# Three fp32 transformer blocks on one core: a second layer begun per channel tile, a convolution slab moved to the matmul engine, and the first network one tile later

## The reference

```python
def first_block(x, ...):
    for i in range(2):                        # layer 0: Hyena, layer 1: RWKV7
        h = _rmsnorm(x, norm_mix_g[i])
        if i % 2 == 0: y = _hyena_mixer(h, ...)
        else:          y, v_first = _rwkv7_mixer(h, v_first, ...)
        x = x + y
        h = _rmsnorm(x, norm_ffn_g[i])
        x = x + _conv_ffn(h, ff_w_up[i], ff_conv_w[i], ff_conv_b[i], ff_w_down[i])
    return _rmsnorm(x, final_norm_g)

def _hyena_filter(...):                       # three layers of 64 channels, then taps for 2 x 1024 channels
    hdn = sin(fq * (z @ w1 + b1)); hdn = sin(fq * (hdn @ w2 + b2)); hdn = sin(fq * (hdn @ w3 + b3))
    k = hdn @ w4; k = k * exp(-t * deltas)

def _rwkv7_mixer(h, ...):
    xx = 0.5 * (h[t - 1] + h[t + 1]) - h      # token difference
    xr, xw, xk, xv, xa, xg = [h + xx * mu[j] for j in range(6)]      # six mixtures
    r = xr @ w_r; k = xk @ w_k; v = xv @ w_v; a = sigmoid(a0 + (xa @ a1) @ a2); ...

def third_block(x, c, ...):
    mod = silu(c) @ w_ada + b_ada             # 6 x 1024 scales and shifts, depends on c alone
    q, k, v, iq, ik, iw, ca, cg = split(h @ w_in)
    attn = dsa_sparse_attention(...)          # 8 heads, 4 blocks of 128 queries, up to 512 keys, top 128 kept
    y = depthwise causal convolution, 31 taps, 512 channels, of ca * sigmoid(cg)
    conv = silu(layer_norm(y))
    x = x + gt1 * (concat[rms_norm(attn), rms_norm(conv)] @ w_out)
    x = x + gt2 * (relu(h2 @ w_ff1) ** 2 @ w_ff2)
```

## Times and profile before

| | us |
|---|---|
| three runs | 3405.93, 3418.65, 3418.45 (median 3418.45) |
| the profiled execution | 3414.19 |
| its span (first to last instruction) | 3412.4 |
| outside the span | 1.8 |
| mean granted clock of PE | 0.956 of full |
| PE busy | 3210.9 (94%) |
| POOL, ACT, DVE busy | 1240.9, 1140.2, 1582.5 |

### The profile page before, as it was taken

How to read it: one execution, slowest core, us unless ns; L and a number is a source line. 1 busy time by engine, 2 the same in 40 slices (tenths; PEclk the granted TensorE clock), 3 DMA queues, 4 the chain that set the end, 5 groups by cost and what they waited for, 6 DMA issues and landing times.

```text
span 3412.4 us, 62787 instructions
## 1 busy us (share of the span) xinstructions
PE 3210.9 (94%) x25578; PEld 2444.1 (72%) x25578; DVE 1582.5 (46%) x2350; ACT 1140.2 (33%) x1619; POOL 1240.9 (36%) x641
## 2 busy tenths in 40 slices
PE   8999999879899999999998999989997998989999
PEld 5757888748688887877766765458885774548887
DVE  6755553284355545777031412353243577436060
ACT  5414433212433333443233223132223235632221
POOL 3323444324034413444433321024442266604443
PEclk9999999989899999999998999999998797699999
DMA  3213333313000002555322321123332120013333
GB/s 134 81 37 93 93 97 102 96 56 99 1 3 3 3 27 73 186 184 184 105 96 74 93 70 54 52 66 95 97 99 68 56 69 31 1 56 99 93 98 99
DMA packets 73073, 266.36 MB, mean 78 GB/s; under 512 B 8207, under 2 KB 8218, under 8 KB 72704
## 3 DMA queue, kind: packets, MB, share of 16 engines
q1 hardware_dynamic: 72000, 260.32, 24.0%
q0 software_dynamic: 896, 3.52, 0.3%
HBM read 261.71 MB, written 2.10 MB: 77 GB/s over the span
## 4 chain that ended last, share of the span: by engine, by line
PE 75%; issue 10%; DVE 7%; POOL 4%; ACT 3%; DMA 0%; SPq 0%; POOLq 0%; DVEq 0%; ACTq 0%
PE gp L388 53%; PE gp L1226 4%; POOL w_low L357 4%; PE gp L314 2%; PE gp L2156 2%; PE gp L2648 2%; PE aux L1343 1%; PE gp L1971 1%; PE aux L1980 1%; PE aux L1226 1%; PE gp L2616 1%; PE aux L565 1%; DVE aux L2812 1%; PE aux L1221 1%; PE aux L2564 1%
## 5 line engine op out<-in xcount | busy, mean ns | idle before, releaser
L357 POOL TENSOR_TENSOR w_low<-ring,w_high 128x1024 fp32r<-128x1024 f32 x397 | 955.2, 2407 | 1774.8 <-ACT w_high L326 1774.8
L326 ACT ACTIVATE w_high<-ring 128x1024 fp32r<-128x1024 f32 x397 | 420.2, 1060 | 1342.5 <-PE gp L388 1291.1
L388 PE MATMUL gp<-ffn_h,w_high 128*128 128x512 f32 x2432 | 757.1, 393 | 12.3 <-DVE ffn_h L418 5.1
L388 PEld LDWEIGHTS gp<-ffn_h,w_high 128*128 128x128 f32 x2432 | 454.7, 188 | 123.3 <-POOL w_low L357 12.0
L388 PE MATMUL gp<-ffn_h,w_low 128*128 128x512 f32 x1216 | 474.7, 390 | 0.0
L388 PE MATMUL gp<-ffn_high,w_high 128*128 128x512 f32 x928 | 362.7, 391 | 9.8 <-POOL w_low L357 9.8
L388 PE MATMUL gp<-ffn_low,w_high 128*128 128x512 f32 x864 | 337.6, 391 | 0.0
L388 PE MATMUL gp<-ffn_high,w_low 128*128 128x512 f32 x864 | 337.2, 390 | 0.0
L388 PEld LDWEIGHTS gp<-ffn_h,w_low 128*128 128x128 f32 x1216 | 229.1, 188 | 48.1
L2084 DVE TENSOR_TENSOR arena<-arena 128x512 f32<-128x512 f32 x64 | 152.6, 2384 | 200.6 <-ACTq L163 200.6
L388 PE MATMUL gp<-in_h,w_high 128*128 128x512 f32 x768 | 239.0, 393 | 4.5 <-DVE in_h L416 4.5
(11 more groups left out here) (466 smaller groups left out, 5144.2 us busy)
## 6 DMA issues: line engine op xcount, KB each, us to landing
ring<-in_weights SPq DMA_DIRECT2D x437, 512.0 KB, 3.6
H<-in_ada SPq DMA_DIRECT2D x48, 512.0 KB, 4.2
X<-in_x SPq DMA_DIRECT2D x4, 512.0 KB, 7.5
out_x<-X SPq DMA_DIRECT2D x8, 256.0 KB, 4.6
arena<-in_sm POOLq DMA_DIRECT2D x1, 1024.0 KB, 5.0
cst<-in_cst SPq DMA_DIRECT2D x1, 756.0 KB, 9.8
arena<-in_hy_f_w POOLq DMA_DIRECT2D x1, 512.0 KB, 5.5
arena<-in_hy_delta POOLq DMA_DIRECT2D x1, 512.0 KB, 6.1
```

What stands on the lines that cost most here:

```text
L326: nc.scalar.activation(w_high[:, slab % PARTS, :], ring[:, slab % RING, :], ACT.Copy).then_inc(high_ready, 1)
L357: nc.gpsimd.tensor_tensor(w_low[:, slab % PARTS, :], ring[:, slab % RING, :], w_high[:, slab % PARTS, :], ALU.subtract).then_inc(low_ready, 1)
L388: last = nc.tensor.matmul(gp[:, t.bank, :], wt[:, slab % PARTS, w], x(k), start=(k == 0 and q == 0), stop=(k == sum(kt) - 1 and q == 2))
```

## The change

Four edits, in four places:

- **A, start.** The sum of squares is read ahead of tile 2 rather than tile 1, the filter network stands ahead of tiles 3, 4, 5 rather than 2, 3, 4. ACT splits two slabs ahead of the root rather than one.
- **B, `down1`.** The squares go to free tiles of `arena` (48 and on) rather than to `H`, and the last four products of `w_ada` stand behind the first four residual additions, one each.
- **C, RWKV7 start.** DVE does for each channel tile its norm, its difference (one copy of two columns rather than two) and its part of mixture 0; PE waits for each tile apart.
- **D, block 3.** The convolution's slab 2 goes to PE: 31 products 128x512 with a diagonal matrix each, which ACT makes from the identity (8 at a time), summed in PSUM bank 2 of `gp`. Four stand ahead of unit 0, two behind each of units 0 to 7, one behind each of units 8 to 18. ACT moves the sum out at unit 20. The list of taps of ACT and POOL is shorter (52 entries rather than 83, POOL's additions 51 rather than 81), one behind each unit, and the scores have two banks rather than three.

```diff
...
             def beside(j):
-                if j == 1:
+                if j == 2:
                     pe.wait_ge(cst_in, 16)
                     folded_norm_pe(pe, arena_tiles(hX1), False)
-                if 2 <= j <= 4:
-                    i = j - 2
+                if 3 <= j <= 5:
+                    i = j - 3
                     if i:
                         pe.wait_ge(f_sin, i)
...
             for t in loop_tiles(act, STAGE["hy_in"], a, body=24):
                 nxt = t.j + 1
-                split_ahead_act(act, t)
+                if t.j != 1:
+                    split_ahead_act(act, t)
                 if t.j == 0:
+                    split_ahead_act(act, Tile(t.st, 1, None, t.body))
                     act.wait_ge(cst_in, 16)
                     root_act(act, a)
...
-                if 2 <= nxt <= 4:
-                    act.wait_ge(f_arg, nxt - 1)
-                    nc.scalar.activation(f_h[nxt - 2], f_t[0], ACT.Sin).then_inc(f_sin, 1)
+                if 3 <= nxt <= 5:
+                    act.wait_ge(f_arg, nxt - 2)
+                    nc.scalar.activation(f_h[nxt - 3], f_t[0], ACT.Sin).then_inc(f_sin, 1)
...
-                if 2 <= t.j + 1 <= 4:
-                    filter_layer(t.j - 1)
+                if 3 <= t.j + 1 <= 5:
+                    filter_layer(t.j - 2)
...
-            squares_beside_act(act, a, f"down{layer}", Xk, Hk, x_wait(act, n_act))
+            squares_beside_act(act, a, f"down{layer}", Xk, arena_tiles(ffX2), x_wait(act, n_act))
...
-            if layer:
-                for j in range(2 * F1T, MODS):
-                    ada_dve(dve, v, j)
-            residual_dve(dve, v, f"down{layer}", sq=Hk)
+            residual_dve(dve, v, f"down{layer}", sq=arena_tiles(ffX2), beside=(lambda j: ada_dve(dve, v, 2 * F1T + j) if j < MODS - 2 * F1T else None) if layer else None)
...
+            for t in loop_tiles(pe, st):
+                bank_wait(pe, t)
+                slab_wait(pe, st.slab0 + t.j)
+                for k in range(DT):
+                    pe.wait_ge(rw_xx, t.j * DT + k + 1)
+                    last = nc.tensor.matmul(gp[:, t.bank, :], ring[:, (st.slab0 + t.j) % RING, k * P:(k + 1) * P],
+                                            arena[:, buf(t.j) + k, :], start=(k == 0), stop=(k == DT - 1))
+                last.then_inc(slab_done, 1)
...
-            pre_norm_dve(dve, v, "norm_mix", DT)
-            v.settle()
-            dve.wait_ge(h_ready, n_dve.h)
+            root_dve(dve, v)
             for i in range(DT):
                 xx, h = arena[:, wXX + i, :], H[:, i, :]
+                nc.vector.scalar_tensor_tensor(out=h, in0=X[:, i, :], scalar=pcol("norm_mix", DT + i), in1=root[:],
+                                               op0=ALU.mult, op1=ALU.mult).then_inc(h_ready, 1)
+                dve.wait_ge(h_ready, n_dve.h + i + 1)
                 v.go(nc.vector.tensor_tensor(xx[:, 1:S - 1], h[:, 0:S - 2], h[:, 2:S], ALU.add))
-                v.go(nc.vector.tensor_copy(xx[:, 0:1], h[:, 1:2]))
-                v(nc.vector.tensor_copy(xx[:, S - 1:S], h[:, S - 2:S - 1]))
+                v(nc.vector.tensor_copy(xx[:, 0:S:S - 1], h[:, 1:S - 1:S - 3]))
                 v(nc.vector.scalar_tensor_tensor(out=xx, in0=xx, scalar=0.5, in1=h, op0=ALU.mult, op1=ALU.subtract))
+                mixed_into(0, i).then_inc(rw_xx, 1)
...
             def score(i):
                 u, n = A.units[i], A.u0 + i
-                if n >= 3:
-                    pe.wait_ge(at_exp, n - 2)
+                if n >= A.banks:
+                    pe.wait_ge(at_exp, n - A.banks + 1)
...
+        DIAGS = 8
+        DIAG_UNIT = lambda u: min(4 + 2 * (u + 1), 20) if u < 8 else min(20 + u - 7, CONVK)
...
+            def tap_products(lo, hi):
+                for k in range(lo, hi):
+                    if k == 0:
+                        pe.wait_ge(cv_pad, 3)
+                    pe.wait_ge(cv_diag, k + 1)
+                    nc.tensor.matmul(gp[:, 2, :], DIAG(k), PE_PAD[:, k:k + S], start=(k == 0), stop=(k == CONVK - 1),
+                                     skip_group_check=True).then_inc(cv_prod, 1)
+            attention_pe(pe, DSA, lambda u: tap_products(0 if u < 0 else DIAG_UNIT(u - 1), DIAG_UNIT(u)))
...
-            attention_act(act, DSA, lambda i: taps(20 + 2 * i, 22 + 2 * i))
-            taps(20 + 2 * len(dsa_units), len(TAPS))
+            def diagonals(lo, hi):
+                for k in range(lo, hi):
+                    if k >= DIAGS:
+                        act.wait_ge(cv_prod, k - DIAGS + 1)
+                    nc.scalar.activation(DIAG(k), ident, ACT.Copy, scale=tap(2, k)).then_inc(cv_diag, 1)
+            def beside(u):
+                taps(20 + u, 21 + u)
+                diagonals(DIAG_UNIT(u) + 2, DIAG_UNIT(u + 1) + 2 if DIAG_UNIT(u + 1) < CONVK else CONVK)
+                if DIAG_UNIT(u - 2) == CONVK > DIAG_UNIT(u - 3):
+                    act.wait_ge(cv_prod, CONVK)
+                    a.go(nc.scalar.activation(arena[:, dCV + 2, :], gp[:, 2, :], ACT.Identity, bias=pcol("b_dw3", 2)))
+                    a.tell(cv_ready)
+            diagonals(0, DIAG_UNIT(0) + 2)
+            attention_act(act, DSA, beside)
+            taps(20 + len(dsa_units), len(TAPS))
...
```

More of the change, by code:

```diff
@@ L638, in h_before, with residual_dve @@
             return before
-        def residual_dve(dve, v, name, bias=None, body=8, sq=None):
+        def residual_dve(dve, v, name, bias=None, body=8, sq=None, beside=None):
             st = STAGE[name]
@@ L652, in residual_dve @@
                 v.tell(drained[t.bank], x_ready)
+                if beside:
+                    beside(t.j)
                 if sq and t.j == DT - 2:
@@ L1958, in build, with __init__, attention_pe @@
         class Attention:
[L1961 removed]
+            def __init__(self, units, p, pt, scale, u0, eye, banks=3):
+                self.banks = banks
                 self.units, self.p, self.pt, self.scale, self.u0, self.eye = units, p, pt, scale, u0, eye
[L1964 removed]
+        def attention_pe(pe, A, beside=None):
             def score(i):
                 u, n = A.units[i], A.u0 + i
[L1967 to L1968 removed]
+                if n >= A.banks:
+                    pe.wait_ge(at_exp, n - A.banks + 1)
                 if u.chosen:
                     pe.wait_ge(sel_ready, u.chosen)
[L1971 removed]
+                nc.tensor.matmul(gp[:, n % A.banks, 0:u.nk], u.q, u.k, start=True, stop=False, skip_group_check=True)
                 lo, m = u.mask
[L1973 removed]
+                nc.tensor.matmul(gp[:, n % A.banks, lo:u.nk], A.eye, m, start=False, stop=True,
                                  skip_group_check=True).then_inc(at_score, 1)
@@ L1985, in attention_pe @@
             score(1)
+            if beside:
+                beside(-1)
             for i, u in enumerate(A.units):
@@ L1997, in attention_pe @@
                     values(i - 1)
+                if beside:
+                    beside(i)
             values(len(A.units) - 1)
@@ L2015, in exp @@
                     act.wait_ge(at_tr, n - 1)
-                nc.scalar.activation(A.p(n)[:, 0:u.nk], gp[:, n % 3, 0:u.nk], ACT.Exp, bias=stat(n, 1),
+                nc.scalar.activation(A.p(n)[:, 0:u.nk], gp[:, n % A.banks, 0:u.nk], ACT.Exp, bias=stat(n, 1),
                                      scale=A.scale if u.root is None else u.root,
@@ L2476, in build @@
         TAPS = [("tap", 0, k, POOL_PAD) for k in range(OWN_TAPS, CONVK - 1)]
-        for _i, _pad in ((3, PAD), (2, POOL_PAD)):
-            TAPS += [("first", _i, CONVK - 1, _pad)] + [("tap", _i, k, _pad) for k in range(CONVK - 1)]
+        TAPS += [("first", 3, CONVK - 1, PAD)] + [("tap", 3, k, PAD) for k in range(CONVK - 1)]
+        cv_diag, cv_prod = f_comb, hy_ready
         def three_pool(pool, g):
@@ L2510, in three_pool @@
                 y = arena[:, dCV + i, :]
-                if (kind, i) == ("first", 3):
-                    pool.wait_ge(cv_used, m)
-                    g.tell(cv_ready)
-                    product(2, POOL_PAD)
-                    g.tell(cv_pad)
-                if (kind, i) == ("first", 2):
+                if m == 6:
+                    pool.wait_ge(in3_ready, in3_at(dCG + 2))
+                    g(nc.gpsimd.memset(PE_PAD[:, 0:CONVK - 1], 0.0))
+                    product(2, PE_PAD)
+                    g.tell(cv_pad)
+                if (kind, i) == ("first", 3):
                     pool.wait_ge(cv_used, m)
```

42 lines of the change are left out of this document (20 added, 22 removed).

## The result

The changed kernel took 3381.83 us (median of four runs, 3377.85 to 3386.75) beside 3417.12 for the kernel before; the ratio is 0.9923, 95% interval 0.9898 to 0.9949. Run once more beside the last experiments it was 3385.33 and the kernel before 3413.02, ratio 0.9918 (0.9897 to 0.9938). The medians lie 35 us apart in the first comparison and 28 in the second; the ratios, which are what the intervals belong to, make it 26 and 28. So it is some 28 us faster, with 7 us either way. The forecast was 20 us faster, 3396, in a range of 3376 to 3425.

The account below looks back on a forecast made before the run. PE, busy 94% of the span, was taken as the bound, through its waits and half-clock stretches. A +5, B -8.7, C -5.5, D -11 sum to -20.2 on 3414.2: 3394.0, stated as 3396, range 3376 to 3425.

Parts of the forecast that it names:

- The clock, on which D hung: Block 3 attention: 31 added products cost 27 us at full or 54 at half clock; filling PE brings full clock back.
- rival 1: Block 3 attention, units 0 to 23, stays at half clock: 54 us on a full engine, total 3463; chance 0.10.
- D's size: Block 3 attention: ACT's copies of the result start at 2965.6 rather than 2976.61, a gain of 11 us.
- its upper end of 14: Block 3 attention: clock full from the first unit, a gain of 14 us.
- the 2.8 us set aside for the last unit and the handovers: End of block 3's attention: 2.8 us for the last unit's own chain and handovers of two banks rather than three.
- The 1.82 and 2.39 us a unit: Block 3 attention: full-clock PE cost per unit of scores, transpositions and values with 256 and 384 keys.
- The cover of about 1 us: `down1`: the weight slab behind `w_ada` 47 is ready at 1648.0, PE wants it at about 1649; uncovered, up to 2.7.
- mixture 3: RWKV7 start: DVE's mixture 3 starts at 708.5 rather than 714.03, and all behind it gains 5.5 us.
- the filter's argument: Hyena start: the filter argument ahead of the sine takes 4.1 us, within PE's predicted wait of 4.9.
- the third sine: Hyena start: the third sine costs another 0.5 us in edit A's sum.
- its 5: Hyena start, edit A: a loss of 5 us, from a sum of 3.7 and 1.7 more if the clock falls.
- The two extra table loads: Hyena start, ACT: sine and exponential alternate; loads cost nothing, as PE's wait or a full tile covers each.

Follow-up runs that it names:

- the kernel without products: Edit D alone with 30 of 31 convolution products and 30 of 31 diagonals left out, against the kernel before: ratio 1.001, 3409.88 us.
- start_2: The full change with DVE's filter argument and ACT's sine one tile earlier; against the kernel before: ratio 0.9953, 3390.12 us.
- the fillers: The full change plus 13 unused products ahead of the sums of block 3's first norm and 3 behind; against the kernel before: 0.9873, 3370.51 us.

## Why the prediction was right, and where it was off

**The clock, on which D hung.** Right, and shown from both sides. The argument was that PE was slow because it was not kept busy, and that products bring the clock. Without them it stays at 0.50 for 70 us and more, with them and nothing else it is full. The 33 busy microseconds at 0.50, which spoke for rival 1, occurred again in the kernel without products (34.70 busy of 34.70 at 0.50), so a full PE in this pattern of small products did not come back for that long; with a 128x512 product or two in each unit it did. What makes the difference between the two was not separated further: the added products are wider, and they also thin out the transpositions. In the attention of block 2, with the same code and no added products, the clock stayed full, so this pattern need not bring it down either; how the clock stood before it seems to count.

**D's size.** 11 predicted for ACT's copies; there it was 12.2 in the full change and 14.8 alone, where the clock was full from the first product (10.6 and 14.8 at low part 334). These are the forecast and its upper end of 14. The diagonals ahead of the first exponential took 2.43 us (2.3 predicted). Smaller terms were off and cancelled: the groups with 256, 384 and 512 keys took 24.9, 24.1 and 24.3 us rather than 23.9, 21.7 and 23.5, and the 2.8 us set aside for the last unit and the handovers lie within these. The 1.82 and 2.39 us a unit that the prediction took for 256 and 384 keys do not follow from the earlier trace rows: halved and divided by 8 units, their busy times give 1.70 and 2.17. Without the convolution's products (17 and 10 records, 8.5 and 5 products of 0.86) the same two windows hold 2.07 and 2.48 after the change.

**B.** 8.7 predicted, 9.0 in both profiles. The slab behind `w_ada` 47 was issued at 1634.12, which is 1641.4 by the time base of before (7.3 us ahead there), as worked out. The cover of about 1 us was mis-sized: the slab reached ACT 4.5 us after its issue rather than 3.6, and PE waited 0.48 us for it. In the seven profiles with B that wait is 0 to 0.5 us, so it cost next to nothing.

**C.** 5.5 predicted, 5.7 in the full change. The mechanism was right: by the time base of before (the changed kernel is 3.8 us late there) PE's second tile ends at 708.2, where 706 to 708.7 was predicted, and mixture 3 starts at 708.3 rather than 708.5. It does so in all seven profiles with C, without a wait for PE. What the prediction took for granted is that all behind mixture 3 gains the same. In five of the seven the clock falls a second time behind it (0.72 rather than 1.00 from 728 to 734 by that base), and from low part 104 on 4.0 to 4.5 us are left of the 5.7.

**A.** The wait appeared where it was named, 3.55 us rather than 4.9. The root was done 1.5 us earlier than worked out (30.3 against 31.8), but PE came 1.3 us earlier too (39.6 against 40.9); what was mis-sized is the filter's argument, 3.1 us (39.18 to 42.3) rather than 4.1, and the third sine cost nothing rather than 0.5. What the prediction could not see in its one profile is that the start has two forms. DVE's last addition of the squares, which PE's sums wait for, takes 0.69 us in the profile before and 2.71 in that of B alone, where POOL had begun a low part ahead of it:

```profile
22.96 0.69 DVE L584 TENSOR_TENSOR arena<-arena 128x512 f32<-128x512 f32 x1
```
```profile
22.87 2.71 DVE L584 TENSOR_TENSOR arena<-arena 128x512 f32<-128x512 f32 x1
```
```profile
25.81 1.19 PE L579 MATMUL aux<-arena,cst 128*128 128x512 f32 x1 [4.61 <-DVEq L163]
```

With the old start the long addition makes PE wait 4.61 and 4.30 us for the sums (B alone, D alone), the clock falls behind that, and low part 8, counted from the first, is 4.5 and 5.0 us later than before; in the six profiles with the short addition the wait is 1.3 to 1.9 us and low part 8 agrees to 0.02. With the new start the long addition is hidden: four profiles have it (the full change twice, start_2, the fillers) and are 1.9 to 2.6 us later than before. The one profile with the new start and the short addition, A alone, is 4.5 later. So A costs about 4.5 us against the form that the prediction was based on, near its 5, and saves about 2.5 against the other. How often each form comes is not known from 13 profiles, and the times say 1.0012 with an interval on both sides of 1. In the two pairs of kernels that differ by A alone on top of the other edits the one with A was even the faster, but not beyond the intervals. It stays open what A costs on average; neither nothing nor 5 us is excluded.

The two extra table loads cost nothing, as priced. Timeline of ACT of the changed kernel at the third sine:

```profile
55.98 1.28 ACT L865 ACT_TABLE_LOAD   x1
57.33 0.63 ACT L865 ACTIVATE arena<-arena 64x512 f32<-64x512 f32 x1
...
59.27 1.28 ACT L848 ACT_TABLE_LOAD   x1
60.56 0.73 ACT L848 ACTIVATE arena<-arena,cst 128x512 f32<-128x512 f32 x1
```

Each function starts right behind its load, 0.07 and 0.01 us after its end. The 1.38 us of draining that the Trainium skill ("ScalarE: Activation LUTs", What ACT_TABLE_LOAD costs) puts on top do not show here; by them A would have cost 7 to 8.

**The time itself.** 3396 was 14 above the measured median. The edits' terms are right within 3 us in sum (22 against 20.2), in part by luck: A came out 3 us better than forecast. What is missing is the base: about 14 us of the difference between the two profiles lie where nothing was edited. The clearest place is block 3's input between low parts 322 and 324, 66 matmul records in every kernel. Before, and in the full change:

```profile
2710.30:2738.20 27.90, 24.17 (x66) 14.61 (x66) 15.04 (x34) 6.14 (x13) 4.79 (x3) 0.69 0.13 39
```
```profile
2690.70:2712.50 21.80, 18.06 (x66) 11.64 (x65) 12.44 (x27) 6.09 (x13) 4.80 (x4) 0.92 0.15 48
```

In the thirteen profiles this stretch took 21.8, 22.5, 27.9 or 29.4 us, with 3.4, 6.8, 17.1 or 20.5 us of it at half clock. Four of the thirteen have 27.9 or more, the kernel before and edit A alone among them. PE is idle for 3.7 us of it in both of these, so the difference is the clock. The whole kernel before varied from 3395.98 to 3426.45 in 26 runs of one group, and in the 23 of another the shortest have a mean clock of 0.961 or 0.962, the longest 0.955. So the one profile on which the sum was based, 3414.19 at 0.956, was at the slow end by its clock, and the first profile of the change was the fastest of its four runs; over all runs the change is some 28 us, not the 36 between the two profiles. Of these 28, the edits' places hold 20 to 22. Whether the rest is chance or a side effect of everything being shifted could not be told apart.

## What to carry to other kernels

Where PE waits in many small pieces, price the clock before the idle time: extra work for PE in the waits can be free, or pay for itself in some of the runs, and moving work onto a busy engine can be faster than leaving it out. Before believing a gain in a place that was not edited, look at the same stretch in several profiles; a forecast from one profile carries that profile's clock. And when the engine held back by a wait is itself in a chain, ask which of the two becomes the bound once both are free, as DVE did here.

## What the runs showed of the hardware

- A TensorE that is busy 34.70 of 34.70 us stayed at the lower level, 1.2 GHz, in the kernel without products and in that of before (0.51 there), with small products between transpositions; the same units with one or two 128x512 products each ran at 2.4 GHz, but for at most 4.8 us behind the first exponential, in every kernel that had these.
- Thirty-one such products, 27 us of work at full clock, added to a 105.5 us stretch shortened it to 95.6 in the profile; the kernel's time stayed the same (ratio 1.0007).
- The same instructions in the same order, 66 records, took from 21.8 to 29.4 us, with 3.7 us of idle time at both ends of that range: the granted clock makes the difference.
- The same DVE addition of 128x512 took 0.69 us in seven profiles and 2.7 to 2.9 us in six, each time with a POOL operation begun ahead of it.
